# Moving the experts' tensors by 416 bytes inside the arena, so that they start at the same place modulo 512 bytes as the weight rings and x

## The chip, the cores and the metric

One core of one Trainium2 chip runs the whole kernel. The metric is the device time of one execution in microseconds (us); the number compared is the median over several executions.

## The reference

Two small transformer stacks run one after the other on x of shape 1 x 256 x 1024, everything in float32. The part that matters here is the mixture of experts at the end of the first stack: a router picks two of eight experts for each token, and every expert is a SwiGLU with 3584 hidden columns.

```
def moe_swiglu(hn, router, w1, w3, w2):
    ...
    logits = (t @ router).astype(jnp.float32)
    top_vals, top_idx = lax.top_k(logits, TOP_K)
    top_w = jax.nn.softmax(top_vals, axis=-1)
    gates = jnp.sum(top_w[..., None] * jax.nn.one_hot(top_idx, N_EXPERTS, dtype=jnp.float32), axis=1)
    out = jnp.zeros_like(t)
    for e in range(N_EXPERTS):
        h_e = jax.nn.silu(t @ w1[e]) * (t @ w3[e])
        out = out + gates[:, e:e + 1].astype(t.dtype) * (h_e @ w2[e])
    return out.reshape(bsz, s, d)
```

Around it stand one even layer (recurrence and attention, then a dense SwiGLU), the odd layer's mixer (gated linear attention), and in the second stack two layers of SwiGLU, a hybrid mixer and SwiGLU again. All weights, 594 MB of them read from memory once, pass through the core.

## The kernel before, in words

**Weights.** Every weight chunk has 128 partitions x 1024 floats (512 KB). SyncE loads it into one of six slots of `RAW`; ScalarE copies it, rounded, into `WHI` (L1421); VectorE writes the rest, raw minus rounded, into `WLO` (L2003). A product is then made of three matmuls: high x high, high x low, low x high. SyncE issues the load of chunk c when VectorE has finished chunk c - 6, ScalarE writes slot c when TensorE has used chunk c - 6, and both convert three chunks ahead of their place in the program.

**The experts.** In the path taken (`moe_sparse`) the up to 128 tokens of an expert are gathered by matmuls with a selection matrix (`PSEL`, L728, for two experts at a time) into `XG`, a high and a low half, two pairs of buffers in turn (`xg0hi`, `xg0lo`, `xg1hi`, `xg1lo`). The hidden columns go in 56 groups of 512 (8 experts x 7). A group G takes 12 weight chunks and runs on TensorE as

- `up_half(G, 0)`: 24 matmuls (L781), gate projection. Stationary is a 128 x 128 piece of `XG`, moving a 128 x 512 piece of `WHI` or `WLO`
- `turn_hidden(G - 1)`: 4 transposes of the previous group's hidden tile (L792)
- `up_half(G, 1)`: 24 matmuls (L781), up projection
- `down_group(G - 1)`: 24 matmuls (L807). Stationary is a piece of `HIDHI` or `HIDLO`, moving is again 512 columns of the rings

The rows of `up_half` look like this:

```
for a, (x, w) in enumerate(((xh, wh), (xh, wl), (xl, wh))):
    last = mm(bank[:, :], x[:, kt, slots], w[:, kk, :],
              start=(kt == 0 and a == 0), stop=(kt == KT - 1 and a == 2))
```

In some groups `aux` puts one or the other small job in the middle of each half: four gather matmuls (L728) for the next two experts, or two matmuls (L737, L738) that spread an expert's output back over the tokens with `PSELT` as stationary and `YEH`, `YEL` as moving operand; in the first expert, transposes of `PSEL`.

**Other matmuls used for comparison.** `unit` makes the projections of the mixers; its row form (L586) has a piece of `XHI` or `XLO` as stationary and 512 columns of the rings as moving operand, and goes through the three products in the same order as L781. `up` (L606, L612) and `down` (L631) belong to the dense SwiGLUs.

**Addresses.** Everything in the on-chip memory is laid out one after the other, in bytes per partition. The raw ring starts at byte 16512, which is 32 x 512 + 128. The rings, x (`X2`), the hidden tiles and the constants have sizes that are multiples of 512 bytes, so each starts at 128 modulo 512. `STAT` has 336 bytes, the arena behind it starts at 464, and `ARENA_AT`, rounded up to 32, at 480 modulo 512. The arena is shared by the stages: each carves its own tensors from its start. The odd layer's carve has 960 words (3840 bytes) ahead of `MOE_OVER`, so `MOE_OVER` lies at 480 + 3840 = 4320, which is 224 modulo 512. From there the mixer's tensors (`OQ`, `OK`, `OV`, `OG` and so on) are carved, and over them, later in time, the experts' tensors: `XG`, `PSEL`, `PSELT`, `YEH`, `YEL`, each a multiple of 512 bytes long. All of them start at 224 modulo 512, and every piece that a matmul takes of them starts at a multiple of 512 bytes from there.

Of the kernel before, what the change touches and what calls it, by code (L numbers as in the profile page):

```python
# [53 lines left out]
def build(nc, A, out):  # L54

    ctx = ExitStack()
    with ctx:
        ctx.enter_context(nc.allow_non_contiguous_dma(reason="small parameter rows"))

        def sb(name, shape, dt=F32):  # L60
            return ctx.enter_context(nc.sbuf_tensor(name, shape, dt))
# [54 lines left out]
        RAW = sb("raw_ring", [P, RING, 1024])  # L116
        WHI = sb("whi_ring", [P, RING, 1024], F32R)
        WLO = sb("wlo_ring", [P, RING, 1024], F32R)
        X2 = sb("x2", [P, KT, 2, S], F32R)
        XHI, XLO = X2[:, :, 0, :], X2[:, :, 1, :]  # L120
        H = sb("h", [P, TT, D])
# [19 lines left out]
        ARENA_AT = -(-nc.sbuf_base // 32) * 32  # L141
# [107 lines left out]
        c = Carve()  # L249
# [16 lines left out]
        c = Carve()  # L266
# [3 lines left out]
               for i, part in enumerate(("hi", "lo"))]  # L270
        c.at += 2 * KT * NE
        LOGT = c(S, parts=NE)
        MOE_OVER = c.at
        OQ, OK, OV, OG = c(4, S), c(4, S), c(2, D), c(2, D)
        LRT = c(S, parts=16)
# [8 lines left out]
        SDEC = c(4, 4)  # L284
        ON = ARENA[:, MOE_OVER:MOE_OVER + 2 * D].rearrange("p (t d) -> p t d", t=TT)
        MSK, POS = c(TT, NE), c(TT, NE)
        FLAG = c(8)
        FLAG_I = FLAG[0:1, 0:1].bitcast(mybir.dt.int32)
        over = [MOE_OVER]

# [11 lines left out]
        SILG, HIDG, HIDGHI, HIDGLO = (x[:, :, :].rearrange("p a b -> p (a b)") for x in (SIL, HID, HIDHI, HIDLO))  # L302
        c.at = over[0] = MOE_OVER
        DSIL, DHID = c(TT, GW), c(TT, GW)
# [7 lines left out]
        c = Carve(ARENA_W)  # L312
# [58 lines left out]
        def wait(eng, name, n):  # L371
            if not isinstance(n, int) or n > 0:
                eng.wait_ge(s[name], n)
# [180 lines left out]
        def _(pe):  # L554
# [4 lines left out]
            def wslot(slot, k):  # L559
                return (WHI[:, slot, :].rearrange("p (k n) -> p k n", k=k),  # L560
                        WLO[:, slot, :].rearrange("p (k n) -> p k n", k=k))

# [5 lines left out]
            def unit(ph, u, lo=0, hi=KT, banks=None):  # L568
# [5 lines left out]
                for i, _, k0, kn in pieces:  # L574
                    c_ = ph["c0"] + i
                    wh, wl = (w[:, c_ % RING, 0:kn * n].rearrange("p (k n) -> p k n", k=kn) for w in (WHI, WLO))
                    for kt in range(max(k0, lo), min(k0 + kn, hi)):
# [16 lines left out]
            def up(c_, slot, q, qb, first, n):  # L594

                wait(pe, "bank_free", q - 1)
                for half in range(2):
# [4 lines left out]
                    def by_high(start, stop):  # L602
                        for kt in range(KT):
                            if first and half == 0:
                                pe.wait_ge(s["x_ready"], nxt("x_ready"))
                            mm_ = mm(bank[:, :], wh[:, kt, :], X2[:, kt, :, :].rearrange("p a n -> p (a n)"),  # L606
                                     start=(start and kt == 0), stop=(stop and kt == KT - 1), skip_group_check=True)
# [15 lines left out]
            def down(c_, slot, t_, b, banks, start=False, stop=False):  # L623

                wait(pe, "lo_ready", c_ + 1)
                wait(pe, "hid_ready", t_ + 1)
                wh, wl = WHI[:, slot % RING, :], WLO[:, slot % RING, :]
                for t, pair in enumerate(banks):
# [25 lines left out]
            def halves(c_):  # L654
                return (WHI[:, c_ % RING, :].rearrange("p (k n) -> p k n", k=2),
                        WLO[:, c_ % RING, :].rearrange("p (k n) -> p k n", k=2))

            def moe_dense():
# [17 lines left out]
                def down(c_, slot, start=False, stop=False):  # L676

                    for j in range(4):
                        pe.wait_ge(s["lo_ready"], c_ + j + 1)
                        wh, wl = WHI[:, (slot + j) % RING, :], WLO[:, (slot + j) % RING, :]  # L680
                        for t in range(TT):
# [36 lines left out]
            def moe_sparse():  # L718
# [76 lines left out]
                def down_group(G, first):  # L795
# [5 lines left out]
                    for j in range(4):  # L801
                        c_ = first + j
                        pe.wait_ge(s["lo_ready"], c_ + 1)
                        wh, wl = WHI[:, c_ % RING, :], WLO[:, c_ % RING, :]
                        for a, (x, w) in enumerate(((HIDGHI, wh), (HIDGHI, wl), (HIDGLO, wh))):
# [291 lines left out]
            def router():  # L1097
# [7 lines left out]
                for t in range(TT):  # L1105
                    last = tr(BANK[3][:, t * NE:(t + 1) * NE], LOGT[:, t * P:(t + 1) * P], IDENT[0:NE, 0:NE])
                last.then_inc(s["score_ready"], 1)
# [881 lines left out]
        def _(dve):  # L1989
# [551 lines left out]
            def router():  # L2541
# [22 lines left out]
                dve.wait_ge(s["score_ready"], 17)  # L2564
                V_.tensor_copy(LOGT[:, :], BANK[2][0:NE, 0:S]).then_inc(s["logit_ready"], 1)
                dve.wait_ge(gbc_full[0], 16)
# [416 lines left out]
```

## Time and profile before

| | |
|---|---|
| Time, median of 3 executions | 2626.16 us (2621.58 to 2626.62) |
| Profiled execution, own time | 2624.73 us |
| Its span | 2622.9 us |
| TensorE busy | 2548.0 us, 97% |
| VectorE / ScalarE busy | 77% / 58% |
| Weight loads of TensorE busy | 82% |
| DMA | 597.24 MB, mean 228 GB/s |
| The experts' 56 groups | 496.98 to 1484.52 us |

The span is the time from the first to the last recorded instruction; the execution's own time holds 1.8 us more. TensorE's matmuls overlap: a row's mean duration is longer than the distance to the next matmul's start, and only that distance says how fast the work goes. The distances can be read from the starts in the timeline or from the lengths of pieces in the chain of work that ended last.

### The profile page before, as it was taken

To read this page: it belongs to the slowest core of one execution; us is meant where nothing else is said; L and a number is where in the kernel's file an instruction comes from. 1 tells how busy PE (TensorE), PEld (TensorE's weight loads), DVE (VectorE), ACT (ScalarE), POOL (GpSimd) and SP (SyncE) were. 2 spreads that over 40 slices of the span, in tenths; PEclk is the share of its full clock that TensorE was granted. 3 is DMA by queue.
4 is the path that set the end of the run, shared out by engine and by line. 5 is a ranking of instruction groups with operands and counts; after the bars stand their busy time and mean duration, and the time that the engine had idled before them with its cause. 6 is when DMAs were issued, how large, how long until landed. Compare 5 with 4: busy or idle time off the path is not lost.

```text
span 2622.9 us, 38439 instructions
## 1 busy us (share of the span) xinstructions
PE 2548.0 (97%) x13856; PEld 2163.7 (82%) x13856; DVE 2016.4 (77%) x2816; ACT 1525.1 (58%) x2090; POOL 63.9 (2%) x137
## 2 busy tenths in 40 slices
PE   9999999899999999999999899999999999999998
PEld 8688887788888888888888788898788888897887
DVE  5566664789898989898999866788766766797665
ACT  5454463577777777777777654532544544623544
POOL 7000000000000000000000000000000000000000
PEclk9899999999999999999999999999999999999999
DMA  7256643499999999999999866532566566413563
GB/s 208 81 164 190 184 138 130 153 363 364 347 355 368 356 349 357 369 345 356 360 366 357 283 196 191 152 89 75 169 192 189 158 190 192 129 59 111 176 192 104
DMA packets 481895, 597.24 MB, mean 228 GB/s; under 512 B 21883, under 2 KB 313155, under 8 KB 481761
## 3 DMA queue, kind: packets, MB, share of 16 engines
q1 hardware_dynamic: 478048, 589.47, 67.5%
q0 software_dynamic: 3712, 6.00, 0.8%
q8 instruction: 81, 1.33, 0.2%
q14 instruction: 54, 0.43, 0.0%
HBM read 594.35 MB, written 1.05 MB: 227 GB/s over the span
## 4 chain that ended last, share of the span: by engine, by line
PE 88%; DVE 8%; ACT 2%; issue 1%; DMA 0%; SPq 0%; DVEq 0%; ACTq 0%
PE bank L781 24%; PE bank L606 16%; PE bank L807 11%; PE bank L631 11%; PE bank L612 8%; PE bank L589 4%; PE bank L586 2%; DVE arena L2718 1%; PE bank L1369 1%; DVE wlo_ring L2003 1%; PE bank L922 1%; PE bank L1091 1%; PE bank L792 1%; PE bank L837 1%; PE bank L728 1%
## 5 line engine op out<-in xcount | busy, mean ns | idle before, releaser
L2003 DVE TENSOR_TENSOR wlo_ring<-raw_ring,whi_ring 128x1024 fp32r<-128x1024 f32 (+1 forms) x1122 | 1328.4, 1220 | 186.2 <-ACT whi_ring L1421 176.5
L1421 ACT CAST whi_ring<-raw_ring 128x1024 fp32r<-128x1024 f32 (+1 forms) x1122 | 1140.9, 1052 | 167.1 <-DMA raw_ring<-in_od_exp_w_dram 153.8
L606 PE MATMUL bank<-x,whi_ring 128*128 128x512 f32 x1760 | 442.8, 393 | 1.0 <-DVE x L2060 1.0
L606 PEld LDWEIGHTS bank<-x,whi_ring 128*128 128x128 f32 x1760 | 323.4, 188 | 69.8 <-DVE x L2060 6.2
L612 PEld LDWEIGHTS bank<-x,wlo_ring 128*128 128x128 f32 x1760 | 225.7, 191 | 8.4
L612 PE MATMUL bank<-x,wlo_ring 128*128 128x256 f32 x1760 | 228.3, 283 | 0.0
L1477 ACT COPY arena<-bank 128x256 f32<-128x256 f32 x110 | 40.9, 372 | 299.2 <-PE bank L612 299.2
L589 PE MATMUL bank<-x,whi_ring 128*128 128x256 f32 (+2 forms) x1024 | 193.6, 290 | 1.0 <-DVE x L2060 1.0
L781 PE MATMUL bank<-whi_ring,xg0hi 128*128 128x512 f32 x448 | 180.3, 402 | 0.3 <-issue 0.3
L781 PE MATMUL bank<-whi_ring,xg1hi 128*128 128x512 f32 x448 | 179.9, 402 | 0.0
L781 PE MATMUL bank<-whi_ring,xg1lo 128*128 128x512 f32 x448 | 177.3, 396 | 0.0
L781 PE MATMUL bank<-whi_ring,xg0lo 128*128 128x512 f32 x448 | 177.3, 396 | 0.0
L781 PE MATMUL bank<-wlo_ring,xg1hi 128*128 128x512 f32 x448 | 177.2, 395 | 0.0
L781 PE MATMUL bank<-wlo_ring,xg0hi 128*128 128x512 f32 x448 | 177.0, 395 | 0.0
L589 PEld LDWEIGHTS bank<-x,whi_ring 128*128 128x128 f32 (+2 forms) x1024 | 156.9, 189 | 8.6 <-issue 5.5
L2078 DVE TENSOR_TENSOR arena<-arena,bank 128x256 f32<-128x256 f32 x110 | 46.3, 421 | 151.0 <-ACT arena L1477 151.0
L589 PE MATMUL bank<-x,wlo_ring 128*128 128x256 f32 (+1 forms) x512 | 145.0, 283 | 0.0
L807 PE MATMUL bank<-whi_ring,hidhi 128*128 128x512 f32 x448 | 139.2, 392 | 1.7 <-DVE hidlo L2195 1.7
L807 PE MATMUL bank<-whi_ring,hidlo 128*128 128x512 f32 x448 | 138.4, 390 | 0.0
L807 PE MATMUL bank<-wlo_ring,hidhi 128*128 128x512 f32 x448 | 138.0, 389 | 0.0
L631 PE MATMUL bank<-whi_ring,hidlo 128*128 128x512 f32 x440 | 135.4, 389 | 0.0
L631 PE MATMUL bank<-wlo_ring,hidhi 128*128 128x512 f32 x440 | 135.4, 389 | 0.0
(492 smaller groups left out, 3508.0 us busy)
## 6 DMA issues: line engine op xcount, KB each, us to landing
raw_ring<-in_od_exp_w_dram SPq DMA_DIRECT2D x672, 512.0 KB, 5.4
raw_ring<-in_ffn_w_gate_dram SPq DMA_DIRECT2D x88, 512.0 KB, 4.0
raw_ring<-in_ffn_w_up_dram SPq DMA_DIRECT2D x88, 512.0 KB, 4.9
raw_ring<-in_ffn_w_down_dram SPq DMA_DIRECT2D x88, 512.0 KB, 3.3
raw_ring<-in_ev_ffn_w_dram SPq DMA_DIRECT2D x66, 512.0 KB, 3.9
raw_ring<-in_w_in_dram SPq DMA_DIRECT2D x42, 512.0 KB, 4.0
raw_ring<-in_od_w_in_dram SPq DMA_DIRECT2D x24, 512.0 KB, 3.9
raw_ring<-in_ev_w_in_dram SPq DMA_DIRECT2D x20, 512.0 KB, 6.3
```

The lines of the kernel that those rows point to most:

```text
L586: last = mm(banks[t] if banks else row_bank(q, n, t), x[:, kt, t * P:(t + 1) * P], w[:, kk, :], start=st and (n > 256 or t == 0), stop=sp_ ...
L589: last = mm(BANK[q % 2][0:n, 0:S], w[:, kk, :], x[:, kt, :], start=st, stop=sp_)
L606: mm_ = mm(bank[:, :], wh[:, kt, :], X2[:, kt, :, :].rearrange("p a n -> p (a n)"), start=(start and kt == 0), stop=(stop and kt == KT - 1 ...
L612: mm_ = mm(bank[:, 0:S], wl[:, kt, :], XHI[:, kt, :], start=(start and kt == 0), stop=(stop and kt == KT - 1), skip_group_check=True)
L631: last = mm(pair[h][:, :], x[:, b, t * P:(t + 1) * P], w[:, h * 512:(h + 1) * 512], start=(start and a == 0), stop=(stop and a == 2), skip ...
L728: last = mm(bank[:, q * S:(q + 1) * S], src[t][:, kt // 2, kt % 2 * P:(kt % 2 + 1) * P], PSEL[:, t, 2 * p:2 * p + 2, :].rearrange("p a b - ...
L781: last = mm(bank[:, :], x[:, kt, slots], w[:, kk, :], start=(kt == 0 and a == 0), stop=(kt == KT - 1 and a == 2))
L807: last = mm(BANK[4 + h][:, :], x[:, j * P:(j + 1) * P], w[:, h * 512:(h + 1) * 512], start=(g == 0 and j == 0 and a == 0), stop=(g == GROU ...
L1421: nc.scalar.copy(WHI[:, slot, 0:n], RAW[:, slot, 0:n]).then_inc(s["hi_ready"], 1)
L1477: nc.scalar.copy(GATE_LO[:, b, :], BANK[2 * b][:, S:2 * S]).then_inc(s["gate_lo"], 1)
L2003: V_.tensor_tensor(WLO[:, slot, 0:n], RAW[:, slot, 0:n], WHI[:, slot, 0:n].bitcast(F32), ALU.subtract)\
L2078: V_.tensor_tensor(GATE[:, qb, :], GATE_LO[:, qb, :], BANK[2 * qb][:, 0:S], ALU.add)\
```

## The change

Ahead of `MOE_OVER` the carve skips as many words as are needed for `MOE_OVER` to lie at the same place modulo 512 as `XHI_AT`, the address of `X2`. (128 - 224) modulo 512 is 416 bytes, 104 words; everything carved for the odd layer after `LOGT` moves up by that. No instruction is added or removed, and no size changes.

```
@@ -116,6 +116,7 @@
         RAW = sb("raw_ring", [P, RING, 1024])
         WHI = sb("whi_ring", [P, RING, 1024], F32R)
         WLO = sb("wlo_ring", [P, RING, 1024], F32R)
+        XHI_AT = -(-nc.sbuf_base // 32) * 32
         X2 = sb("x2", [P, KT, 2, S], F32R)
         XHI, XLO = X2[:, :, 0, :], X2[:, :, 1, :]
         H = sb("h", [P, TT, D])
@@ -270,6 +271,7 @@
                for i, part in enumerate(("hi", "lo"))]
         c.at += 2 * KT * NE
         LOGT = c(S, parts=NE)
+        c.at += (XHI_AT - ARENA_AT - 4 * c.at) % 512 // 4
         MOE_OVER = c.at
         OQ, OK, OV, OG = c(4, S), c(4, S), c(2, D), c(2, D)
         LRT = c(S, parts=16)
```

## Rows read from the trace of the kernel before

**Rows 1.** The experts' stretch by windows: busy time, instructions, granted clock, DMA share, GB/s.
```profile
core 0: us, PE busy (x) PEld busy (x) DVE busy (x) ACT busy (x) POOL busy (x), PEclk, DMA share, GB/s
496.98:1484.52 987.54, 985.82 (x4424) 803.38 (x4424) 889.54 (x841) 751.45 (x813) 0.00 (x0) 1.00 0.98 356
```

**Rows 2.** The chain that ended last, two groups without a small job: start, length.
```profile
561.62 5.62 PE bank L781 x24
567.24 0.44 PE bank L792 x4
567.67 5.62 PE bank L781 x24
573.29 5.48 PE bank L807 x24
578.77 5.61 PE bank L781 x24
```

**Rows 3.** The same chain in a group with gathers.
```profile
666.30 2.81 PE bank L781 x12
669.11 0.48 PE bank L728 x4
669.59 2.80 PE bank L781 x12
684.35 2.81 PE bank L781 x12
```

**Rows 4.** Timeline of TensorE, gate half of one group: start, duration, line.
```profile
561.69 0.39 PE L781 MATMUL bank<-wlo_ring,xg0hi 128*128 128x512 f32 x1
...
566.61 0.39 PE L781 MATMUL bank<-wlo_ring,xg0hi 128*128 128x512 f32 x1
```

**Rows 5.** Timeline of TensorE, a projection in the odd mixer.
```profile
378.75 0.39 PE L586 MATMUL bank<-wlo_ring,x 128*128 128x512 f32 x1
...
385.56 0.39 PE L586 MATMUL bank<-wlo_ring,x 128*128 128x512 f32 x1
```

**Rows 6.** Timeline of TensorE, the down projection behind an up half.
```profile
573.13 0.63 PE L807 MATMUL bank<-whi_ring,hidhi 128*128 128x512 f32 x2
...
574.98 0.61 PE L807 MATMUL bank<-wlo_ring,hidhi 128*128 128x512 f32 x2
...
578.61 0.39 PE L781 MATMUL bank<-whi_ring,xg0hi 128*128 128x512 f32 x1
```

**Rows 7.** Timeline of TensorE, a dense SwiGLU's down projection.
```profile
265.67 0.62 PE L631 MATMUL bank<-whi_ring,hidhi 128*128 128x512 f32 x2
...
268.39 1.98 PE L606 MATMUL bank<-x,whi_ring 128*128 128x512 f32 x8
```

**Rows 8.** Groups of TensorE's instructions in the experts' stretch (one of six L781).
```profile
L781 PE MATMUL bank<-whi_ring,xg0hi 128*128 128x512 f32 x448 | 180.3, 402 | 0.3 <-issue 0.3
L792 PE MATMUL bank<-ident,hid 128*128 128x128 f32 x224 | 33.5, 272 | 0.0
L728 PE MATMUL bank<-psel,x 128*128 128x256 f32 x96 | 15.3, 280 | 0.0
```

**Rows 9.** Waits in the experts' stretch: us in total, times, longest.
```profile
PE bank L807 <- DVE hidlo L2195: 1.7, 1, 1.7
ACT whi_ring L1421 <- DMA raw_ring<-in_od_exp_w_dram: 149.9, 327, 3.0
```

**Rows 10.** Windows of the experts' stretch, columns as in rows 1.
```profile
1060.00:1065.00 5.00, 5.00 (x25) 4.09 (x24) 3.95 (x5) 4.17 (x6) 0.00 (x0) 1.00 1.03 411
792.00:877.00 85.00, 85.00 (x378) 69.05 (x377) 75.98 (x71) 64.93 (x69) 0.00 (x0) 1.00 1.00 366
1056.00:1124.00 68.00, 68.00 (x303) 55.25 (x302) 61.17 (x57) 53.42 (x56) 0.00 (x0) 1.00 1.01 372
```

**Rows 11.** The chain at the end of the experts' stretch.
```profile
1463.95 1.18 PE bank L781 x5
...
1469.60 6.18 DMA raw_ring<-in_od_exp_w_dram
...
1478.77 5.75 PE bank L807 x24
```

More of the change, by code:

```diff
@@ L118, in build @@
         WLO = sb("wlo_ring", [P, RING, 1024], F32R)
+        XHI_AT = -(-nc.sbuf_base // 32) * 32
         X2 = sb("x2", [P, KT, 2, S], F32R)
@@ L272, in build @@
         LOGT = c(S, parts=NE)
+        c.at += (XHI_AT - ARENA_AT - 4 * c.at) % 512 // 4
         MOE_OVER = c.at
```

## The prediction

> **What bounds the kernel now.** I read the page first: TensorE is busy 97% of the span. The change touches only tensors of the odd layer, so I cut out the stretch that uses them most, the 56 groups of the experts. By windows it is 987.54 us long, TensorE is busy 985.82 us of it at full granted clock, the DMA share is 0.98 and VectorE is busy 889.54 us [rows 1]. The list of waits agrees: TensorE waits 1.7 us in all, once, at the very end [rows 9]. So in this stretch the time is the number of matmuls by the distance between their starts, and DMA stands close behind.
>
> The chain of waits shows the pattern of a group: 5.62 + 0.44 + 5.62 + 5.48 us, a period of 17.15 us (561.62 to 578.77) [rows 2]. The reader should see that 24 matmuls of L781 take 5.61 or 5.62 us while the 24 of L807, of the same shape, take 5.48. The timeline gives the distances. L781 goes from 561.69 to 566.61 in 21 matmuls (one of every three is a low-ring one, seven steps), 234.3 ns each [rows 4]. L807 needs 1.85 us for its first eight (231.3 ns each) and 3.63 us for the other sixteen (226.9 ns each) [rows 6]. L631 makes twelve in 2.72 us, 226.7 ns each [rows 7].
>
> The best comparison is L586. It has the same three products in the same order, a 128-column stationary and a 512-column moving operand and one bank at a time, as L781 has; its stationary is x, which lies at 128 modulo 512, where L781's lies at 224. From 378.75 to 385.56 it makes thirty matmuls, 227.0 ns each [rows 5]. L807 and L631 also take their stationary from a tile at 128. So what sets L781 apart is not the alternation of operands, nor the stage with its DMA and VectorE traffic (L807 runs at 226.9 in the middle of that), and the address of the stationary is what is left. A table of busy times would mislead: L781's mean of 402 ns [rows 8] overlaps the next matmul.
>
> **The change part by part.** Nothing is removed or added; 416 bytes of padding bring `XG`, `PSEL`, `PSELT`, `YEH` and `YEL` from 224 to 128 modulo 512.
>
> Step 1, L781. Its six groups of 448 are 2688 matmuls [rows 8]. I take the value of L586, 227.0 instead of 234.3 ns, 7.3 ns less per distance. Distances that begin a run behind another line stay as they are: 55 behind the transposes L792 (224 / 4 = 56 blocks, of which the last is followed by L807), 24 behind gathers (96 / 4 [rows 8]) and 4 behind the transposes of `PSEL` (two groups of the first expert, two halves), 83 in all. (2688 - 83) x 7.3 ns = 19.0 us. Bounds: below, nothing (the address has no effect); above, L631's 226.7 instead of 227.0, 0.8 us more.
>
> Step 2, the run-in. L807's first eight distances are 8 x (231.3 - 226.9) = 0.035 us too long [rows 6], whereas L606 behind L631 and L631 itself show none (2.72 us for twelve from the first on [rows 7]). I read it as the stream settling after a different one. If L781 then has L807's address and rhythm, L807 follows without a run-in: 56 x 0.035 = 2.0 us gained. In return the runs of L781 behind transposes and gathers get one of their own: 83 x 0.035 = 2.9 us lost. Bounds: without either part 0, with only one of them 2.0 gained or 2.9 lost. The expert outputs through L737 and L738 are two 512-column matmuls with operands that also come to 128; 28 pairs at most, I cost them at nothing (at 7.3 ns each they would give 0.4 us).
>
> Step 3, the gather L728 has x as stationary and `PSEL` as moving operand, 0.48 us for four [rows 3]: 96 of them, even 3 ns each would be 0.3 us. ScalarE's and VectorE's copies into `XG`, `YEH` and `YEL` are few and lie under TensorE's work. The odd mixer's tensors move by the same 416 bytes; its path is mostly projections with x and the rings, which don't move. Nothing for all of these; between 1 us gained and 1 us lost.
>
> Step 4, what a faster TensorE triggers. Ring slots come free earlier, so the weights must come at a higher rate. A group without a small job would take 17.15 - 2 x 0.175 - 0.035 + 0.035 = 16.80 us for twelve chunks of 0.524 MB, 374.5 GB/s; one with gathers or outputs is about 0.9 us longer (684.35 - 666.30 = 18.05 us now [rows 3]), about 17.7 us after, 355 GB/s. By the places in the program half of the groups, 28, are of the second kind, so the mean need is 356 x 987.54 / (987.54 - 18.1) = 363 GB/s. The trace shows 366 over 85 us, 372 over 68 us and 411 in a window of 5 us [rows 10], with TensorE never waiting. ScalarE does wait for DMA, 149.9 us in 327 waits [rows 9], but it runs up to three chunks ahead of use, 3 x 1.4 us, and the longest stretch of groups without a small job is six: even if DMA gave no more than 12 chunks in 17.15 us, it would fall behind by 6 x 0.35 = 2.1 us, less than that lead, and catch up by 17.15 against 17.7 in the next groups. I cost this at nothing; were the cover gone, it is rival B.
>
> Step 5, the end of the stretch. The last down group waits for a chain from L781 (1463.95) over a load of 6.18 us to 1478.77 [rows 11]. It hangs on L781 and so moves ahead with it as a whole, at its present length; only one L807 run before it lies beside the chain. Zero, at most 1 us lost.
>
> Sum: 19.0 + 2.0 - 2.9 = 18.1 us. Against the profiled execution that is 2624.7 - 18.1 = 2606.6 us; its time is 1.4 us under the median of the runs shown, so the median should come to 2626.2 - 18.1 = 2608.1, say 2608 us.
>
> The Trainium skill speaks against a gain. Its page SBUF — State Buffer, section Who interferes with whom, gives TensorE two independent read ports, one for the moving operand and one for weight loads, and says that TensorE never waits on anyone; the page's 16-byte cachelines divide 224 as well as 128. By that the start would not matter and the sum would be 0, 2626 us. By the rows above it is 7.3 ns a matmul and 18.1 us.
>
> **The rivals.**
>
> A, no change. L781's 7.3 ns come from something other than the address: a cause that L586, L807 and L631 all lack, such as the experts' buffers being written by ScalarE and VectorE from the bank shortly before. Against it: the distance is the same in groups where nobody writes `XG` (5.62 us [rows 2]) and where somebody does (2.81 for twelve [rows 3]). Or the chip cares for another modulus or for which two addresses meet, and 128 against 128 only looks good by chance of slot. Against that speak three lines. Time 2626 us, chance 9%.
>
> B, DMA takes part of it. If the memory can't give the 363 GB/s on average, TensorE waits. At the 356 of now as a cap the gain is nil. I take a cap in the middle between the mean of now and what is needed, 360: the stretch then takes 987.54 x 356 / 360 = 976.6 us, 11 us gained, 2615 us. For it speaks the DMA share of 1.00 [rows 10] and ScalarE's 327 waits; against it 372 GB/s over 68 us without a wait of TensorE. Chance 9%. By the 358 GB/s that the same page of the Trainium skill states for memory to core (section A bandwidth-pool intuition that's wrong (but worth ruling out)) the stretch would take 982 us and the kernel 2621 us; this trace has exceeded that figure over 85 us.
>
> C, slower. The stationary pieces now start at the same place modulo 512 as the moving ones. If that made the two reads of TensorE meet instead of avoiding each other, every distance of L781 would rise. It decides from 2 ns on (2605 x 2 ns = 5.2 us); with 4 ns, as far above the present 234.3 as the worst that I would expect from a run-in that never settles, the cost is 10 us and the time 2636 us. Against it: L586, L807 and L631 all have both operands at the same place and are the fastest of their shape [rows 5, 6, 7]. Chance 3%.
>
> **How the numbers follow.** The forecast (all or nearly all of step 1) has 79%; its own range is 2604 to 2612, from the bounds of steps 1 and 2 (+0.8, +2.9, -2.0), of steps 3 and 5, and a us or two for the median of few executions, which spread over 5 us here. To leave out no more than 2 in 10 the range reaches to rival B and a little above, and below for executions like the fastest shown: 2602 to 2617. Faster or slower by 0.2%, 5.2 us, is about what a measurement of this kernel can tell from no change. Faster: the forecast and most of B, 0.87. Same: A and the rest of B, 0.10. Slower: C, 0.03.
>
> **What would show it.** Right: in the chain the pieces of L781 x24 have 5.44 to 5.48 us instead of 5.62, those of L807 x24 5.44 instead of 5.48, and a group without a small job 16.8 us; the timeline of L781 shows 227 ns from start to start after the first eight. The projections L586 and the dense stages stay as they are. Step 4 is right if TensorE's waits stay at one or two us and the windows show 363 GB/s or more; rival B shows as waits of L781 or L807 for VectorE's low halves with DMA behind them. Rival A shows as an unchanged 5.62. The prediction goes wrong above all if the distance depends on something in the pairing of addresses that 128 against 128 in L586 doesn't cover.

## The result

The changed kernel takes 2610.38 us (median of 6, 2605.93 to 2613.97) against 2626.24 us before (median of 6). The ratio is 0.9935, 95% interval 0.9922 to 0.9949. By the ratio that is 17 us faster, and between 13 and 20 at the interval's ends; the two medians lie 15.9 us apart. The forecast was 18.1 us less, 2608 us. The profiled execution took 2605.93 us, the shortest of the six; its span fell from 2622.9 to 2604.1 us, by 18.8.

The experts' stretch by windows, to be compared with [rows 1], comes first. All later line numbers are 2 higher than before: L783 is the up half, L809 the down group, L794 the transposes.

```profile
496.83:1466.91 970.08, 968.61 (x4424) 802.03 (x4424) 888.94 (x841) 753.89 (x814) 0.00 (x0) 1.00 1.00 362
```

The stretch has the same 4424 matmuls and is 17.46 us shorter (987.54 to 970.08). TensorE is still busy all of it, and VectorE's and ScalarE's work is what it was. The other 1.3 us of the span lie outside: 0.15 ahead of the stretch, 1.2 behind it, too little to tell from noise.

The chain that ended last, in the same part of the stretch as [rows 2]:

```profile
560.33 5.44 PE bank L783 x24
565.77 0.44 PE bank L794 x4
566.21 5.49 PE bank L783 x24
571.70 5.44 PE bank L809 x24
577.14 5.44 PE bank L783 x24
```

A group takes 16.81 us (560.33 to 577.14) instead of 17.15. The half that follows a down group takes 5.44 instead of 5.62; the half behind the transposes 5.49 and in the next group 5.47; the down group 5.44 instead of 5.48.

The timeline of TensorE for a down group and the half behind it, to be compared with [rows 4] and [rows 6]:

```profile
554.73 0.62 PE L809 MATMUL bank<-whi_ring,hidhi 128*128 128x512 f32 x2
...
556.54 0.62 PE L809 MATMUL bank<-wlo_ring,hidhi 128*128 128x512 f32 x2
...
560.16 0.39 PE L783 MATMUL bank<-whi_ring,xg0hi 128*128 128x512 f32 x1
560.39 0.39 PE L783 MATMUL bank<-wlo_ring,xg0hi 128*128 128x512 f32 x1
...
565.15 0.39 PE L783 MATMUL bank<-wlo_ring,xg0hi 128*128 128x512 f32 x1
```

From 560.39 to 565.15 L783 makes 21 matmuls, 226.7 ns each; 234.3 before. And L809's first eight now take 1.81 us (554.73 to 556.54) instead of 1.85: the run-in, the slightly longer distances at the start of a stream, is gone there.

### The profile page after: what moved, and what is told of

Read it like the earlier page. It is cut to its first block, busy times and chain, and to the rows that moved or that the text cites. A ratio compares the mean times of both kernels' runs of the same rounds, so it can differ in the third digit from the quotient of the medians.

```text
span 2604.1 us, 38439 instructions
## 1 busy us (share of the span) xinstructions
PE 2529.0 (97%) x13856; PEld 2160.4 (83%) x13856; DVE 2015.5 (77%) x2816; ACT 1527.2 (59%) x2090; POOL 64.1 (2%) x137
## 4 chain that ended last, share of the span: by engine, by line
PE 89%; DVE 8%; ACT 1%; issue 1%; DMA 0%; DVEq 0%; ACTq 0%
PE bank L783 24%; PE bank L608 16%; PE bank L809 12%; PE bank L633 11%; PE bank L614 8%; PE bank L591 4%; PE bank L588 2%; DVE arena L2720 1%; PE bank L1371 1%; PE bank L845 1%; PE bank L839 1%; DVE wlo_ring L2005 1%; PE bank L924 1%; PE bank L794 1%; PE bank L1093 1%
## 5 line engine op out<-in xcount | busy, mean ns | idle before, releaser
L1423 ACT CAST whi_ring<-raw_ring 128x1024 fp32r<-128x1024 f32 (+1 forms) x1122 | 1143.2, 1053 | 167.6 <-DMA raw_ring<-in_od_exp_w_dram 152.5
L783 PE MATMUL bank<-whi_ring,xg0hi 128*128 128x512 f32 x448 | 177.7, 397 | 0.1
L783 PE MATMUL bank<-whi_ring,xg1hi 128*128 128x512 f32 x448 | 177.2, 396 | 0.0
L783 PE MATMUL bank<-whi_ring,xg0lo 128*128 128x512 f32 x448 | 174.9, 390 | 0.0
L783 PE MATMUL bank<-whi_ring,xg1lo 128*128 128x512 f32 x448 | 174.8, 390 | 0.0
L783 PE MATMUL bank<-wlo_ring,xg0hi 128*128 128x512 f32 x448 | 174.8, 390 | 0.0
L783 PE MATMUL bank<-wlo_ring,xg1hi 128*128 128x512 f32 x448 | 174.6, 390 | 0.0
L809 PE MATMUL bank<-whi_ring,hidhi 128*128 128x512 f32 x448 | 138.0, 389 | 1.4 <-DVE hidlo L2197 1.4
L809 PE MATMUL bank<-wlo_ring,hidhi 128*128 128x512 f32 x448 | 138.0, 389 | 0.0
L809 PE MATMUL bank<-whi_ring,hidlo 128*128 128x512 f32 x448 | 137.9, 389 | 0.0
L633 PE MATMUL bank<-whi_ring,hidhi 128*128 128x512 f32 x440 | 135.5, 389 | 0.0
```

The source lines that it names most:

```text
L633: last = mm(pair[h][:, :], x[:, b, t * P:(t + 1) * P], w[:, h * 512:(h + 1) * 512], start=(start and a == 0), stop=(stop and a == 2), skip ...
L783: last = mm(bank[:, :], x[:, kt, slots], w[:, kk, :], start=(kt == 0 and a == 0), stop=(kt == KT - 1 and a == 2))
L809: last = mm(BANK[4 + h][:, :], x[:, j * P:(j + 1) * P], w[:, h * 512:(h + 1) * 512], start=(g == 0 and j == 0 and a == 0), stop=(g == GROU ...
L1423: nc.scalar.copy(WHI[:, slot, 0:n], RAW[:, slot, 0:n]).then_inc(s["hi_ready"], 1)
```

## The experiments

The change satisfies two theories at once. Theory P: what counts is the distance, modulo some length, between the places of TensorE's two operands. Theory Q: what counts is the place of the stationary operand alone. The prediction named Q's cause ("the address of the stationary is what is left"), used P's only against its rival C, and named the pairing of the two addresses as the way in which it could go wrong. Each run is compared with executions of the kernel before on the same chip.

**1. All tensors at 224 modulo 512.**

```
+        sb("pad", [P, 24])
         RAW = sb("raw_ring", [P, RING, 1024])
```

(The arena is 96 bytes shorter, which nothing used.)

> 96 bytes of padding ahead of the raw ring: rings, x, the hidden tiles, the constants and the experts' tensors all start at 224 modulo 512, so stationary and moving operands still have the same place. Theory P (only the distance between the places of the stationary and of the moving operand counts): as the changed kernel, 2610 us, up halves 5.44 to 5.47 us in the chain. Theory Q (the stationary itself has to start at a boundary that 128 is on and 224 is not): every matmul with 512 columns slows by 7.3 ns, some 7700 of them, 56 us, so 2666 us, and the dense down projection takes 5.6 us per 24 instead of 5.44.

Measured: 2613.43 us, ratio 0.9943 (0.9925 to 0.9960). The chain, dense SwiGLU and experts:

```profile
267.39 2.72 PE bank L634 x12
...
562.20 5.44 PE bank L784 x24
...
573.57 5.44 PE bank L810 x24
```

All the gain of the change is there with every operand at 224. Whether the common place is 128 or 224 does not matter. Q falls.

**2. x, the hidden tiles and the experts' tensors 96 bytes from the rings.**

```
+        sb("pad", [P, 24])
         XHI_AT = -(-nc.sbuf_base // 32) * 32
         X2 = sb("x2", [P, KT, 2, S], F32R)
```

> 96 bytes of padding between the rings and x: rings at 128 modulo 512, x, the hidden tiles and the experts' tensors at 224. Theory P: all pairs of operands with a ring are now 96 bytes apart, as the experts' were before, some 7700 matmuls by 7.3 ns, 56 us, so 2666 us. Theory Q: only those whose stationary lies at 224, without the 1760 of the dense up projection that have a ring piece as stationary, 43 us, so 2653 us, and the dense up projection stays at 227 ns. A third theory, that it never was the address but something in the experts' buffers: 2626 us, dense stages unchanged.

Measured: 2656.06 us, ratio 1.0104 (1.0071 to 1.0137). The chain, dense up, dense down, experts' up and down:

```profile
268.62 1.87 PE bank L609 x8
270.49 2.81 PE bank L634 x12
273.29 1.87 PE bank L609 x8
...
574.30 5.61 PE bank L784 x24
579.91 5.63 PE bank L810 x24
585.54 5.62 PE bank L784 x24
```

The dense down projection takes 2.81 us where it took 2.72 [rows 7], the experts' down group 5.63 instead of 5.44. The dense up projection has the ring piece as stationary and x as moving operand, and it rises too, to 1.87 us per eight. In run 1 it takes 1.81 us behind the down projection and 1.84 behind L615:

```profile
261.83 1.81 PE bank L609 x8
...
265.55 1.84 PE bank L609 x8
...
270.11 1.81 PE bank L609 x8
```

So it is the pair, whichever of the two is the stationary one. The 256-column matmuls of the dense up projection show no clear price: sixteen of L615 take 1.92 us here and 1.91 in run 1.

The median is 45.7 us above the changed kernel's, below the 56 expected. The expectation took 7.3 ns for each of some 7700 matmuls. Added up along the chain of this run and of the changed kernel, the dense up projection takes 417.3 instead of 408.4 us, the dense down 302.5 instead of 293.8, the experts' down 315.1 instead of 305.0 and the experts' up 628.7 instead of 612.8. That is 43.6 us for 7112 matmuls, 6.1 ns each. It leaves about 2 us of the measured difference for the mixers, which is too little to tell from noise. The direction is P's, and the expected size was too high because the price of one row was taken for all.

**3. Only the gathered x at the rings' place.** The selection matrices and the experts' outputs lie 96 bytes apart.

```
         XG = [[rounded(f"xg{b}{part}", KT, 2 * P) for part in ("hi", "lo")] for b in range(2)]
+        over[0] += 24
```

> The gathered x at 128 modulo 512, the selection matrices and the experts' outputs back at 224. Both theories: the whole gain stays, 2610 us; up halves 5.44 to 5.47 us, at most 1 us lost by the gathers and the spreading of the outputs. Rival (the padding helps elsewhere, in the mixer or the small jobs): up halves as in the changed kernel but a time visibly above it.

Measured: 2612.76 us, ratio 0.9938 (0.9920 to 0.9955); up halves of 5.44 and 5.49 us.

**4. Everything but the gathered x at the rings' place.**

```
+        over[0] += 24
         XG = [[rounded(f"xg{b}{part}", KT, 2 * P) for part in ("hi", "lo")] for b in range(2)]
+        over[0] += 104
```

> The gathered x back at 224 modulo 512, the selection matrices and the experts' outputs at 128. Both theories: no gain is left, 2626 us, up halves 5.61 us; at most 1 us better through the 28 pairs of output matmuls.

Measured: 2628.45 us, ratio 1.0000 (0.9984 to 1.0016); up halves of 5.61 us:

```profile
571.55 5.61 PE bank L785 x24
...
577.61 5.61 PE bank L785 x24
```

In run 4 the mixer's tensors are where the change puts them, and so are the selection matrices and outputs; together they give at most 4 us, the half width of the interval, and 0 at its centre. The gain belongs to the operand of L783.

**5 to 8. Other distances**, in four kernels and a fifth that fills in the row. The two pairs of buffers, `xg0` (experts 0, 1, 4, 5) and `xg1` (2, 3, 6, 7), get distances of their own from the rings' place:

```
-        XG = [[rounded(f"xg{b}{part}", KT, 2 * P) for part in ("hi", "lo")] for b in range(2)]
+        XG = []
+        for b, apart in enumerate((128, 256)):
+            over[0] += apart // 4
+            XG.append([rounded(f"xg{b}{part}", KT, 2 * P) for part in ("hi", "lo")])
+            over[0] += (512 - apart) % 512 // 4
```

> The first pair of gathered-x buffers lies 32 bytes behind the rings' place modulo 512, the second pair 64 bytes. Theory P with 512 bytes as the length that counts: both pairs run at about 234 ns a matmul, as at 96 bytes; time about 2626 us. Theory P with a shorter length, 64 or 32 bytes: the pair at 64 bytes (or both) runs at 227 ns; time 2617 us or less.

> First pair 128 bytes behind the rings' place, second pair 256 bytes. Theory P with 512 bytes: both at about 234 ns, 2626 us. With 128 bytes as the length: both at 227 ns, 2609 us. With 256 bytes: only the second pair at 227 ns, 2618 us.

> First pair 192 bytes, second pair 320 bytes behind the rings' place. Theory P with 512 bytes: both at about 234 ns, or a price that changes evenly with the distance, highest in the middle. With 64 bytes as the length both at 227 ns.

> First pair 384 bytes, second pair 480 bytes behind the rings' place (that is 128 and 32 bytes ahead of it). Theory P with 512 bytes: both at about 234 ns if any distance costs the same; if only the stationary lying behind the moving operand costs, these two are at 227 ns.

> First pair of gathered-x buffers 160 bytes, second pair 224 bytes behind the rings' place, to fill in the row of distances. With 256 bytes as the length, 224 is the same as the 480 of the run before and should take 233.1 ns; 160 lies between 128 (232.8 ns) and 192 (229.1 ns), so 229 to 233 ns. Time 2624 to 2628 us.

The cut shown is that for 128 and 256 bytes; the others differ in the two numbers. One execution each: 2630.42, 2620.28, 2627.45, 2627.64 and 2623.04 us. Single times don't separate these kernels; the chain's pieces do. With 128 and 256 bytes, first in expert 0, then in expert 2:

```profile
570.74 5.58 PE bank L787 x24
...
576.76 5.57 PE bank L787 x24
```

```profile
816.09 5.44 PE bank L787 x24
...
821.97 5.47 PE bank L787 x24
```

One and the same kernel has 5.58 us in the buffers at 128 bytes and 5.44 in those at 256, so no difference between two kernels enters the comparison. With 192 (expert 0) and 320 bytes (expert 2):

```profile
570.55 5.50 PE bank L787 x24
...
576.48 5.51 PE bank L787 x24
```

```profile
815.97 5.60 PE bank L787 x24
...
822.01 5.60 PE bank L787 x24
```

All distances, as the length of 24 matmuls of the up half in the chain (first half / half behind the transposes):

| bytes from the rings' place | us per 24 |
|---|---|
| 0 | 5.44 / 5.47 or 5.49 |
| 32 | 5.59 / 5.61 |
| 64 | 5.60 |
| 96 (kernel before) | 5.61 / 5.62 |
| 128 | 5.58 / 5.57 to 5.59 |
| 160 | 5.60 |
| 192 | 5.50 / 5.51 |
| 224 | 5.58 to 5.60 |
| 256 | 5.44 / 5.47 or 5.49 |
| 320 | 5.60 |
| 384 | 5.58 / 5.57 to 5.59 |
| 480 | 5.58 to 5.60 |

The row repeats after 256 bytes wherever both were measured: 0 and 256, 64 and 320, 128 and 384, 224 and 480 agree in pairs. The first pair carries the weight, for the other three lie so close together (5.57 to 5.60) that they could not tell one period from another. So the length that counts is 256, not the 512 of the change. The price does not grow with the distance: 32 bytes cost almost as much as 96, and 192 bytes cost only a third. 448 bytes, the partner of 192, was not measured.

**9. 160 bytes of padding.**

```
-        c.at += (XHI_AT - ARENA_AT - 4 * c.at) % 512 // 4
+        c.at += (XHI_AT - ARENA_AT - 4 * c.at) % 256 // 4
```

> 160 bytes of padding instead of 416: the experts' tensors lie 256 bytes from the rings' place modulo 512. Theory P with 256 bytes as the length that counts: as the changed kernel, 2610 us, up halves 5.44 to 5.49 us. Theory P with 512 bytes and some other reason for the good second pair of the run before (experts 2, 3, 6, 7 against the others): the first pair stays near 233 ns, 2618 us.

Measured: 2610.92 us, ratio 0.9930 (0.9905 to 0.9955), up halves mostly 5.44 us, and 5.47 to 5.49 behind the transposes. The 256 extra bytes of the change buy nothing.

**10. All pairs 256 bytes apart.** As run 2, with a pad of 64 words ahead of x instead of 24.

> 256 bytes of padding between the rings and x: x, the hidden tiles and the experts' tensors all 256 bytes from the rings' place. Theory P with 256 bytes: as the changed kernel, 2610 us, dense up and down projections at 227 ns and 5.44 us. Theory P with 512 bytes: slower in all stages as with 96 bytes between them, about 2656 us.

Measured: 2612.52 us, ratio 0.9935 (0.9912 to 0.9959), up halves 5.44 and 5.49 us:

```profile
570.31 5.44 PE bank L784 x24
...
576.20 5.49 PE bank L784 x24
581.69 5.44 PE bank L810 x24
```

Run 2 and this one differ only in the pad between the rings and x, 96 or 256 bytes, and lie 43.5 us apart. In the dense SwiGLU, too, eight of L609 take 1.81 or 1.84 us here and twelve of L634 2.72, as in run 1.

**11. How far away is the next bound?** The up halves of the changed kernel leave out the third product, low half of gathered x by high half of the weights. (`stop` moves to the second product.)

```
-                            for a, (x, w) in enumerate(((xh, wh), (xh, wl), (xl, wh))):
+                            for a, (x, w) in enumerate(((xh, wh), (xh, wl))):
```

> On top of the changed kernel the up halves leave out the third product, low half of gathered x by high half of the weights (16 matmuls instead of 24 per half), so TensorE needs only about 13.1 us per group, and the next bound shows. If DMA can give no more than 360 GB/s (rival B), a group takes 17.5 us, the stretch stays at 970 us and the time at 2610 us. If DMA has the head room that I assumed, VectorE is next with 12 x 1.22 + 1.4 = 16.1 us per group: the stretch takes about 900 us, at 390 GB/s, and the time is about 2543 us.

Measured: 2585.62 us in one execution, neither of the two. By windows (columns as in [rows 1]) and in the list of waits of TensorE, its weight loads and ScalarE:

```profile
500.00:1440.00 940.00, 857.28 (x3520) 612.05 (x3519) 887.53 (x839) 757.25 (x812) 0.00 (x0) 0.99 1.01 374
```

```profile
ACT whi_ring L1423 <- DMA raw_ring<-in_od_exp_w_dram: 170.1, 456, 1.9
PEld bank L783 <- DVE wlo_ring L2005: 154.2, 219, 2.2
PE bank L783 <- DVE wlo_ring L2005: 59.0, 117, 1.8
```

TensorE lost 56 x 16 x 227 ns = 203 us of work, and this one execution is about 25 us faster than the changed kernel's median. The chain shows what closes the loop, once per group:

```profile
566.75 3.51 DVE wlo_ring L2005 x3
570.28 5.56 DMA raw_ring<-in_od_exp_w_dram
575.86 1.07 ACT whi_ring L1423
576.95 1.24 DVE wlo_ring L2005
578.19 0.04 issue
578.23 1.20 PE bank L783 x4
```

VectorE frees a raw slot, the load into it takes 5.56 us, then come the two conversions, and TensorE waits for them. The stretch moves 374 GB/s over 940 us and 391 from 562 to 630. VectorE is busy 887.53 of the 940 us, 94%, so this run does not show memory alone to be the next bound; it shows the loop of loads, conversions and ring slots.

## Why the prediction was right

**Step 1, L781 falls to L586's distance.** Right in the number: 226.7 ns in the timeline against 227.0 forecast (the bound of 226.7 was named). The cause that the step rests on, the address of the stationary operand, was wrong. Run 1 puts that operand at 224, where L781 had been slow, and keeps the gain; runs 2 and 10 show that the distance to the other operand decides, runs 5 to 10 that its length is 256 bytes. All matmuls used for comparison had both operands at 128, so their rows could not tell the two causes apart. The change made both true at once, and so the number came out right for either; that much was luck. A change that had only rounded the experts' tensors to a boundary of 128 bytes could have missed the gain (128 bytes apart: 5.58 us).

**Step 2, the run-in changes its place.** Right in both parts: L809 has none (1.81 us for its first eight), and the halves behind the transposes have 5.47 or 5.49 us instead of 5.44, 0.03 to 0.05 where 0.035 was put.

**Step 3, nothing elsewhere.** Right within 4 us, by run 4: without the gathered x the ratio is 1.0000 (0.9984 to 1.0016).

**Step 4, the weights come fast enough.** Right. Two windows of the changed kernel (the second is in [rows 10]; the first held 303 matmuls and 368 GB/s before), with TensorE's waits and ScalarE's beside them:

```profile
562.00:630.00 68.00, 68.00 (x309) 56.18 (x307) 62.41 (x59) 54.79 (x59) 0.00 (x0) 1.00 1.02 377
792.00:877.00 85.00, 85.00 (x389) 70.36 (x387) 78.00 (x73) 67.53 (x73) 0.00 (x0) 1.00 1.02 377
```

```profile
PE bank L809 <- DVE hidlo L2197: 1.4, 1, 1.4
```

```profile
ACT whi_ring L1423 <- DMA raw_ring<-in_od_exp_w_dram: 152.5, 351, 2.1
```

The need of 363 GB/s on average is met (362 in the stretch), 377 over 85 us, and TensorE's only wait of the stretch is still the one at its end. ScalarE's waits for DMA went from 149.9 to 152.5 us, in 351 instead of 327 places. The Trainium skill's figure for memory to core, 358 GB/s, which would have held the stretch at 982 us (SBUF — State Buffer, section A bandwidth-pool intuition that's wrong (but worth ruling out)), is passed by these rows and by run 11. But the head room was smaller than the prediction made it sound: by the one execution of run 11 the whole of it is some 25 us of the kernel.

**Step 5, the end of the stretch.** The forecast of zero, at most 1 us lost, was right within 0.3 us, though the picture of the chain was not: the load of [rows 11] is no longer in it.

```profile
1459.31 0.45 PE bank L794 x4
1459.78 0.59 ACT hidhi L1580
1460.40 0.70 DVE hidlo L2197
1461.15 5.76 PE bank L809 x24
```

TensorE, ScalarE and VectorE follow one another. What that is worth is read from TensorE's wait ahead of its last down group, 1.7 us before [rows 9] and 1.4 now, and not from the length of the load, 6.18 us, most of which TensorE had worked through. It is not an effect of the change: runs 3 and 9 have the whole gain and the load in the chain, run 4 has no gain and no load there.

**The sum** of 18.1 us compares with 17.5 in the stretch and 18.8 in the span of the profiled executions, and with 17 us by the ratio. The median came 2.4 us above the forecast; the executions of one kernel spread over 8 us here, so that can be noise.

**The rivals.** A (no change) and C (operands at the same place collide) are out. So is what the Trainium skill's SBUF — State Buffer, section Who interferes with whom, would have made of the time: its two read ports of TensorE may be independent, but runs 2 and 10, 43.5 us apart by a pad alone, show that two operands of TensorE do slow each other when their places are 96 bytes apart and not when they are 256. B took nothing here; run 11 shows loads in the loop that bounds the stretch next.

What stays open is the mechanism underneath. The runs show the price by distance; they don't show why 192 bytes cost a third of the rest, nor what the two reads share.

## What to carry to other kernels

Where TensorE bounds a stage and matmuls with 512 columns follow one another, compare the distance between starts of lines of the same shape: 227 against 234 ns is a defect, and 7.3 ns by the number of matmuls is what it costs. The mean durations (402, 396 and 395 ns for L781's operands before, 397, 390 and 390 now) give a hint of it, but they overlap, so no time can be added up from them. Then put stationary and moving operands a multiple of 256 bytes from each other (shown here with 512 columns, at distances of 0 and 256, and for a common place of 128 and of 224); the odd-sized tensor laid out ahead of them (here 336 bytes of `STAT` and what the carve holds before `MOE_OVER`) is what breaks it. Before hoping for more from a faster TensorE, leave out a part of its work once: it shows in one run how far the next bound is.

## What the runs showed of the hardware that I had not expected

- Stationary and moving pieces whose starts lie 32, 64, 96, 128, 160 or 224 bytes apart cost 5.57 to 5.61 us per 24 matmuls with 512 columns (5.62 in places at 96), 192 bytes 5.50, and 0 bytes 5.44; 0 and 256 are alike (runs 5 to 8 and 10), and a common place of 128 or of 224 gives the same time (run 1).
- In the changed kernel a half behind the transposes takes 5.47 or 5.49 us, 0.03 to 0.05 more than one behind a down group (5.44). L807 behind the slower L781 spent such a surplus in its first eight matmuls (1.85 us against 1.81); behind the faster L783 it has none.
- In run 11 one core read 374 GB/s over 940 us and 391 over 68 us, in chunks of 512 KB. At 391 GB/s the 5.56 us of one load are time for four such chunks, so several were on the way at a time.
